# First loads reordered at the start of a two-block fp32 kernel, and the taps of the first four convolved channel pairs moved later

## What is computed

```python
def conv_ffn(hn, w_ffn_in, conv_w, conv_b, w_ffn_out, valid):
    l = hn.shape[1]
    u = jnp.where(valid[None, :, None], hn @ w_ffn_in, 0.0)
    up = jnp.pad(u, ((0, 0), (CONV_W - 1, 0), (0, 0)))
    c = conv_b + sum(conv_w[j] * up[:, j:j + l] for j in range(CONV_W))
    gate, val = jnp.split(c, 2, axis=-1)
    return (jax.nn.silu(gate) * val) @ w_ffn_out
...
    for li in range(DEPTH):
        lambda_init = 0.8 - 0.6 * math.exp(-0.3 * li)
        h = h + mixer(rms_norm(h, norm_mix_g[li]), w_in[li], w_branch[li], w_out[li], lbs[li],
                      da_lambda[li], da_subln_g[li], lambda_init, valid, pos)
        h = h + conv_ffn(rms_norm(h, norm_ffn_g[li]), w_ffn_in[li], ffn_conv_w[li], ffn_conv_b[li],
                         w_ffn_out[li], valid)
```

## Time and profile before

| | us |
|---|---|
| median of the three runs | 2747.8 |
| lowest and highest of the three | 2744.36, 2748.49 |
| the profiled execution, its own time | 2745.64 |
| its span in the trace | 2743.8 |

### The profile page before, as it was taken

The page is one execution under the profiler, slowest core; times in us unless marked ns, Lnnn a source line. Parts: engine busy times, 40 slices in busy tenths (PEclk is TensorE's granted clock), DMA queues, the critical chain, the costliest instruction groups (busy, mean ns, idle before and its releaser), DMA issues.

```text
span 2743.8 us, 49227 instructions
## 1 busy us (share of the span) xinstructions
PE 2569.7 (94%) x19196; PEld 2384.6 (87%) x19196; DVE 1468.5 (54%) x2672; ACT 1348.5 (49%) x2339; POOL 1985.1 (72%) x2181
## 2 busy tenths in 40 slices
PE   6889999998999999999998999978989998998999
PEld 6889888898999888889898998677879998778999
DVE  5876432358736874333458744645355436764540
ACT  4434444555654534445455645551255445564543
POOL 6966556797989966558798988250059999566997
PEclk8999999999999999999999999998999999999999
DMA  6433334444655433334455775120026665333665
GB/s 199 132 88 100 108 101 125 126 144 137 186 172 157 139 93 101 108 108 133 118 166 147 212 199 136 42 86 7 1 72 191 185 185 154 90 92 109 187 187 154
DMA packets 682934, 354.90 MB, mean 129 GB/s; under 512 B 11121, under 2 KB 680913, under 8 KB 682321
## 3 DMA queue, kind: packets, MB, share of 16 engines
q1 hardware_dynamic: 680464, 343.45, 43.6%
q10 hardware_dynamic: 2240, 8.31, 0.9%
HBM read 350.67 MB, written 1.05 MB: 128 GB/s over the span
## 4 chain that ended last, share of the span: by engine, by line
PE 71%; DVE 11%; POOL 8%; ACT 4%; issue 3%; DMA 2%; ACTq 0%; DVEq 0%
PE pb L276 70%; POOL wl L345 8%; ACT pool L299 1%; DVE bx L655 1%; ACT wh L334 1%; DVE xl L784 1%; DMA raw<-in_w_in 1%; DVE pool L1078 1%; PE pb L553 0%; DVE bx L790 0%; DMA raw<-in_w_ffn_in 0%; DVE bx L3265 0%; DMA raw<-in_ffn_w 0%; DVE pool L952 0%; PE pb L1309 0%
## 5 line engine op out<-in xcount | busy, mean ns | idle before, releaser
L345 POOL TENSOR_TENSOR wl<-raw,wh 128x256 fp32r<-128x256 f32 (+1 forms) x2164 | 1973.9, 948 | 748.8 <-ACT wh L334 747.5
L276 PE MATMUL pb<-xh,wh 128*128 128x272 f32 (+2 forms) x3104 | 940.9, 303 | 26.2 <-DVE pool L494 5.1
L334 ACT ACTIVATE wh<-raw 128x1024 fp32r<-128x1024 f32 (+2 forms) x669 | 689.7, 1033 | 451.6 <-PE pb L276 310.0
L276 PE MATMUL pb<-xh,wl 128*128 128x272 f32 (+2 forms) x3104 | 891.0, 287 | 0.0
L276 PE MATMUL pb<-xl,wh 128*128 128x272 f32 (+2 forms) x3104 | 891.0, 287 | 0.0
L276 PEld LDWEIGHTS pb<-xh,wh 128*128 128x128 f32 x3104 | 592.7, 191 | 52.5 <-issue 19.2
L276 PEld LDWEIGHTS pb<-xl,wh 128*128 128x128 f32 x3104 | 593.2, 191 | 3.3
L276 PEld LDWEIGHTS pb<-xh,wl 128*128 128x128 f32 x3104 | 592.2, 191 | 0.0
L276 PE MATMUL pb<-pool 128*128 128x128 f32 (+15 forms) x2064 | 325.5, 305 | 38.0 <-DVE pool L1078 14.6
L276 PEld LDWEIGHTS pb<-pool 128*128 128x128 f32 (+6 forms) x2064 | 237.6, 176 | 104.2 <-DVE pool L1078 19.8
L276 PE MATMUL pb<-u2h,wh 128*128 128x256 f32 x840 | 242.3, 288 | 5.5 <-DVE u2l L647 5.0
(11 more groups left out here) (374 smaller groups left out, 3826.7 us busy)
## 6 DMA issues: line engine op xcount, KB each, us to landing
raw<-in_w_in SPq DMA_DIRECT2D x208, 512.0 KB, 3.7
raw<-in_ffn_w SPq DMA_DIRECT2D x120, 512.0 KB, 3.8
raw<-in_w_ffn_in SPq DMA_DIRECT2D x88, 512.0 KB, 3.8
raw<-in_w_branch SPq DMA_DIRECT2D x48, 512.0 KB, 3.6
raw<-in_od_w_in SPq DMA_DIRECT2D x41, 512.0 KB, 3.8
raw<-in_w_ffn_out SPq DMA_DIRECT2D x32, 512.0 KB, 3.8
raw<-in_ev_w_in SPq DMA_DIRECT2D x20, 512.0 KB, 3.9
raw<-in_w_out SPq DMA_DIRECT2D x16, 512.0 KB, 3.6
```

What stands on the lines that cost most here:

```text
L276: return e.matmul(out, lhsT=l, rhs=r, start=a, stop=z, skip_group_check=True)
L334: E.e.activation(hi, src, ACT.Copy).then_inc(*sig("weight_hi", ("hi", g)))
L345: E.e.tensor_tensor(lo[:, s, :], src[:, s, :], hi[:, s, :].bitcast(F32), SUB).then_inc(*sig("weight_lo", *[("lo", g, i) for i in ks]))
```

## The change

At the start: the third weight piece no longer waits for `h`. Of the constants only the first three matrices (identity, ones, blocks of ones; 384 columns) are loaded at first, and the vectors right behind them; both stand ahead of the split of piece 1. The split of piece 2 moves to the middle of the squares. Lambda, the other constants (2689 columns) and the masks are requested within `a_scalars`, one at each step, and DVE turns the masks into bytes at the end of `v_scalars` instead of at its beginning, with waits `in_l` and `in2` of their own.

In each feed-forward stage of block one: for the first eight pieces there is only the scaled copy, into eight slots (`GS`, and the buffer `pbuf`); kind `cfirst`. Their taps, sigmoid, products and splits are side work `later`, in slots of their own in `rsb`, taken at rate 0.15 from the ninth piece on, four steps for each pair, sixteen in all.

```diff
@@ sp_project @@
-            if g == 2:
-                e.wait_ge(*at("in", 1))
@@ a_all_made @@
-        e.dma_start(cst[:, :], A["consts"]).then_inc(*landed("in_c", ("in_c",)))
+        c0 = cplan["p1"][0]
+        e.dma_start(cst[:, 0:c0], A["consts"][:, 0:c0]).then_inc(*landed("in_c"))
+        e.dma_start(vec[:, 8:], A["vecs"][:, 8:]).then_inc(*landed("in_c", ("in_c",)))
         a_split(E, 1)
-        e.dma_start(vec[:, 8:], A["vecs"][:, 8:]).then_inc(*landed("in2"))
-        e.dma_start(lam_in, A["lam"].broadcast_to([P, 512])).then_inc(*landed("in2"))
-        e.dma_start(POOL[:, 12288:12288 + MASKS * P], A["masks"]).then_inc(*landed("in2", ("in2",)))
-        a_split(E, 2)
         for k in range(8):
+            if k == 4:
+                a_split(E, 2)
@@ a_scalars @@
         a_logsig(E, lbt[:, 5, :], lbt[:, 0, :], "sc_a", ("sc", "l1"))
+        e.dma_start(lam_in, A["lam"].broadcast_to([P, 512])).then_inc(*landed("in_l", ("in_l",)))
         yield
         e.wait_ge(*at("sc", "m1"))
         a_logsig(E, lbt[:, 5, :], lbt[:, 4, :], "sc_a", ("sc", "l2"))
-        yield
+        c0 = cplan["p1"][0]
+        e.dma_start(cst[:, c0:], A["consts"][:, c0:]).then_inc(*landed("in2"))
+        yield
+        e.dma_start(POOL[:, 12288:12288 + MASKS * P], A["masks"]).then_inc(*landed("in2", ("in2",)))
         yield
@@ the feed-forward stage @@
+    LATER = 4
+    FIRST = [GS, PB[:, :, :].rearrange("p a b -> p (a b)").rearrange("p (a b) -> p a b", b=NT)]
+    LG, LS, LV, LP = (RSb[:, i * NT:(i + 1) * NT] for i in range(4))
+    def v_later(E, name, conv):
+        for j in range(LATER):
+            for what, dst, ch in (("g", LG, j), ("v", LV, HID // P + j)):
+                o = FIRST["gv".index(what)][:, j, :]
+                e.wait_ge(*at("tap2", name + what, j))
+                e.scalar_tensor_tensor(out=dst[:, 1:NT], in0=o[:, 0:NT - 1], ..., in1=dst[:, 1:NT], ...)
+                e.wait_ge(*last("later_v"))
+                e.scalar_tensor_tensor(out=dst[:, 2:NT], in0=o[:, 0:NT - 2], ..., in1=dst[:, 2:NT], ...)
+                yield
+            e.wait_ge(*at("gate_s", name, j))
+            e.tensor_tensor(LP, LG, LS, MLT)...
+            e.wait_ge(*last("later_v"))
+            e.tensor_tensor(LV, LV, LP, MLT)...
+            yield
+            e.wait_ge(*at("hh", name, j))
+            e.tensor_tensor(HIDL[:, j, :], LV, HIDH[:, j, :].bitcast(F32), SUB)...
+            yield
+    def v_cfirst(E, p, j, r, g):
+        v_scaled(E, p, j, r, g, FIRST["gv".index(p.name[-1])][:, j, :], ("scaled", p.name, j))
@@ glu @@
+            if conv and a == 512:
+                E.credit, later = 0.0, E.bg("later", name, conv)
+            E.run(E.part["project"](E, Proj(name + "g", ..., gate, conv=conv, **aux)), later, 0.15)
+            E.run(E.part["project"](E, Proj(name + "v", ..., val, conv=conv, **aux)), later, 0.15)
```

More of the change, by code:

```diff
@@ L1729, in program, with a_later @@
     GS = pv(20000, [4, NT])
+    LATER = 4
+    FIRST = [GS, PB[:, :, :].rearrange("p a b -> p (a b)").rearrange("p (a b) -> p a b", b=NT)]
+    LG, LS, LV, LP = (RSb[:, i * NT:(i + 1) * NT] for i in range(4))
+    def a_later(E, name, conv):
+        e, (cw, cb) = E.e, conv
+        for j in range(LATER):
+            if j:
+                e.wait_ge(*at("l_gate", name, j - 1))
+            for what, dst, ch in (("g", LG, j), ("v", LV, HID // P + j)):
+                e.wait_ge(*at("scaled", name + what, j))
+                if what == "v" and j:
+                    e.wait_ge(*at("lo_done", name, j - 1))
+                act(E, dst, FIRST["gv".index(what)][:, j, :], ACT.Identity, scale=vc(cw, 3 * ch + 2), bias=vc(cb, ch)).then_inc(
+                    *sig("later_a", ("tap2", name + what, j)))
+                yield
+            e.wait_ge(*at("taps", name + "g", j))
+            act(E, LS, LG, ACT.Sigmoid).then_inc(*sig("later_a", ("gate_s", name, j)))
+            yield
+            e.wait_ge(*at("hid", name, j))
+            e.activation(HIDH[:, j, :], LV, ACT.Copy).then_inc(*sig("later_a", ("hh", name, j)))
+            yield
@@ L1741, in v_taps @@
         e, (cw, cb) = E.e, p.aux["conv"]
-        o, freed = banks[r % 3], (("out", r),)
-        if p.aux["scaled"]:
-            v_scaled(E, p, j, r, g, GS[:, s, :], ("scaled", p.name, j))
-            e.wait_ge(*last("out_v"))
-            o, freed = GS[:, s, :], ()
+        o = banks[r % 3]
         e.wait_ge(*at("tap2", p.name, j))
@@ L1751, in v_taps @@
         e.scalar_tensor_tensor(out=dst[:, 2:NT], in0=o[:, 0:NT - 2], scalar=vc(cw, 3 * ch), in1=dst[:, 2:NT], op0=MLT,
[L1752 removed]
+                               op1=ADD).then_inc(*sig("taps", ("out", r), ("taps", p.name, j)))
     def a_cgate(E, p, j, r, g):
         name, q = p.name[:-1], j % 2
[L1756 removed]
+        if j >= LATER + 2:
             E.e.wait_ge(*at("gate", name, j - 2))
@@ L1869, in glu @@
         Wv = W.rearrange("(k p) c -> p k c", p=P)
-        E.rest, E.lo, E.conv = [], [], conv is not None
+        E.rest, E.lo, E.conv, later = [], [], conv is not None, None
         c = "c" if conv else ""
@@ L1877, in glu @@
             aux["dense"], aux["t0"] = a >= 512, t0
-            E.run(E.part["project"](E, Proj(name + "g", Wv, 8, a, 256, a // P, n, x, c + "gate", conv=conv, scaled=scaled, **aux)))
-            E.run(E.part["project"](E, Proj(name + "v", Wv, 8, HID + a, 256, a // P, n, x, c + "val", conv=conv, scaled=scaled, **aux)))
+            gate, val = ("cfirst", "cfirst") if conv and scaled else (c + "gate", c + "val")
+            if conv and a == 512:
+                E.credit, later = 0.0, E.bg("later", name, conv)
+            E.run(E.part["project"](E, Proj(name + "g", Wv, 8, a, 256, a // P, n, x, gate, conv=conv, **aux)), later, 0.15)
+            E.run(E.part["project"](E, Proj(name + "v", Wv, 8, HID + a, 256, a // P, n, x, val, conv=conv, **aux)), later, 0.15)
+        if later is not None:
+            drain(later)
         E.do("glu_end", name)
```

45 lines of the change are left out of this document (28 added, 17 removed).

## The result

The changed kernel takes **2733.96 us** (median of 15 runs, 2724.45 to 2745.71), the kernel before 2749.44 us on the same chips (15 runs, 2743.71 to 2760.21). The ratio is **0.9946, 95% interval 0.9932 to 0.9959**: 14.8 us faster, 11.3 to 18.7. The forecast was a gain of 29.3 us, to 2718.5. The profiled execution took 2729.2 us with a span of 2727.3, 16.5 us less than the earlier trace rows.

The account below looks back on a forecast made before the run. PE's matmuls were taken as the bound, gains only where PE waits or clocks lower. 10.3 + (13.2 - 2.3) + (15.3 - 7.2) = 29.3 us gained, to 2718.5 us; range 2706 to 2738.

Parts of the forecast that it names:

- Reading the kernel: Whole kernel: PE has matmuls for 2569.7 of 2743.8 us, so gains come only where it stands or clocks lower.
- The start: Program start: third weight piece requested at once, PE's sum of squares at 18.5 instead of 28.85 us, gain 10.3 us.
- The first pieces: First eight pieces of block one's feed-forward stages: only scaled copies stay, gaining 13.2 us in layer 0, 15.3 in layer 1.
- the last line of the prediction: Signs of error: moved instructions over 1.2 us, a weight piece late at 25 to 40 us, POOL pacing the first pieces.
- The later work: Dense feed-forward pieces: 28 moved DVE instructions a stage take 21.8 us, costing 2.3 us in layer 0, 7.2 in layer 1.
- were all at 1.06, 29.7: Upper bound for DVE's moved work in a dense stage: every tap and product at 1.06 us, 29.7 us in all.
- The room: DVE's idle time in dense pieces: 0.5 us a piece in layer 0, 0.33 in layer 1, plus two pieces of lateness.
- Half a POOL instruction each: Rival, dense pieces: every moved instruction waits half a POOL instruction, 1.2 us each, 33.6 a stage; 2742 us, 8%.
- Slower: Rival, dense pieces: each moved instruction waits a whole POOL instruction, 1.53 us; 2760 us, deciding from 1.30 us each; 4%.
- Long stalls move: Rival: DVE stalls like the 10.69 us one at 109.30 vanish (2711, 10%) or come among the later work (2726, 12%).
- Constants starve the weights: Rival, start: late constant and mask loads delay weight pieces by 4.3 us, or up to 12; 2723 to 2730 us, 13%.
- the start alone works: Rival: only the start gains, the taps' cost equalling their gain in the feed-forward stages; 2737 us, 3%.

Follow-up runs that it names:

- the one with PSUM: Changed kernel with the two tiles in which the moved taps are built put in free PSUM banks instead of SBUF: 2717.56 us, ratio 0.9879.
- the trace with the held tap: First trace of the changed kernel, nothing else altered, in which one moved tap of layer 1 took 7.19 us; profiled execution 2729.2 us.
- the second trace: The changed kernel run and traced once more, nothing altered: 2731.18 us, ratio 0.9934.
- the kernel with half of POOL's columns: Changed kernel with POOL forming low halves of only 64 of 128 columns per weight piece in block one's dense feed-forward pieces: 2710.99 us, ratio 0.9846.

## Why the prediction was wrong where it was

**Reading the kernel: right.** PE was the bound, and both places that the change attacks gave what stood there. The sum's matmul came at 18.65 us (18.5 forecast), no wait of ACT for a weight piece was above 1.84 us until 48 us, and PE's waits for L494 went.

**The start: right in size, and its reason narrower than told.** 10.3 us forecast, 10.0 to 11.5 in the traces at 40 us; nearly all of it is SP's wait. No trace shows a cost of the late loads. By its own runs the start alone is worth 7.1 (3.6 to 10.7) us.

**The first pieces: a little less.** 13.2 and 15.3 us forecast, 11.8 to 13.1 and 13.0 to 13.8 measured (9.5 in the trace with the held tap). In layer 0 most of the missing 1.4 us is PE at 1.2 GHz for 3.4 us from 617.1 us, after it has waited 1.1 us for the norm's sum: where the clock stays high after that wait the gain is 13.0 to 13.1. In layer 1 POOL, never idle, sets the pace, as the last line of the prediction feared: between 1418.95 and 1425.7 PE's matmuls, 0.12 us apart, come late fourteen times, by 0.07 to 0.16 us, 1.4 us together. That is inside the 0 to 1.5 us given for it (in layer 0).

**The later work: the step that failed.** "16 x 0.57 + 12 x 1.06 = 21.8 us" took the taps from the earlier trace rows and the products from the earlier trace rows. Measured were 1.15 for a tap and 1.05 for a product in layer 0, 30.9 us. The taps of the earlier trace rows were cheap because POOL had gaps where they stood, since PE waited there. The trace of before, DVE's timeline and then POOL's:

```profile
631.91 0.86 DVE L1751 SCALAR_TENSOR_TENSOR pool<-pool,vec 128x270 f32<-128x270 f32 x1
...
642.08 0.50 DVE L1751 SCALAR_TENSOR_TENSOR pool<-pool,vec 128x270 f32<-128x270 f32 x1
```

```profile
627.86 13.88 POOL L345 TENSOR_TENSOR wl<-raw,wh 128x256 fp32r<-128x256 f32 x17
642.78 3.39 POOL L345 TENSOR_TENSOR wl<-raw,wh 128x256 fp32r<-128x256 f32 x4 [1.05 <-ACT wh L334]
```

The four taps that began before 641.5, beside POOL's run without a gap, took 0.62, 0.86, 0.83 and 0.86 us, although POOL's instructions were the shorter ones there; the other twelve took 0.50 each, as POOL stood for 1.05 to 3.06 us between two pieces. The mean of 0.57 mixed the two. The moved ones stand where POOL is busy for 93 of 107 us. The products' row, beside it, had the right price for both, and the prediction's own bound "were all at 1.06, 29.7" would have been the value to take. The argument used against it, that a tap of 0.56 shows taps to be cheap, compared two conditions and not two instructions.

The room was mis-sized the other way. DVE's idle time over the whole dense part, in windows of before, of the changed kernel and of the one with PSUM:

```profile
672.00:774.00 102.00, 101.77 (x807) 101.80 (x808) 78.33 (x124) 64.18 (x105) 98.07 (x72) 1.00 0.62 180
```

```profile
650.00:757.00 107.00, 103.24 (x798) 102.09 (x797) 102.63 (x143) 67.13 (x116) 93.16 (x67) 0.98 0.56 163
```

```profile
655.00:754.00 99.00, 97.98 (x773) 97.33 (x772) 94.96 (x145) 63.74 (x111) 86.97 (x64) 1.00 0.59 169
```

The third figure is DVE's: before it was idle for 23.7 of 102 us, 0.70 a piece (807 matmuls are 33.6 pieces of 24), not 0.5; after for 4.4 of 107. Put right, the prediction's sum is 30.9 - 27 x 0.70 - 6.0 = 6.0 us lost in layer 0; measured 6.7 and 8.0. In layer 1 (19.5 us idle in 33.9 pieces, 0.575) it is 36.4 - 15.5 - 5.7 = 15.2, in the second trace, with 33.1 us of moved work, 11.9; measured 8.2 and 8.6 against the trace of before, which itself loses at least 4.7 us there, as the kernel with half of POOL's columns shows (PE waits 2.40 and 0.48 us at 1521.22 and 1529.28 and runs for 3.4 us at its lower clock): 12.9 and 13.3. The form of the sum holds within 2.3 us, its price did not.

So of the 12.8 us missing in the profiled execution (29.3 - 16.5) layer 0 has 5.8 (10.9 forecast, 5.1 measured), 4.4 of it the price of the later work and 1.4 the first pieces. Layer 1 has 6.8 (8.1 against 1.3), 5.8 in the stretch called first, of which some 3.6 is the held tap by the traces that lack it (13.0), and 1.0 in the dense one. The rest balances: the start stretch gave 1.1 more, the other stages took 1.3.

**The rivals.** *Half a POOL instruction each* had the price, 1.2 against 1.11 and 1.30, by luck in part as told above, and was given 8%; its 2742 was too slow since its room was too small. *Slower* did not come: its point was 1.30 us an instruction, and layer 1 reached just that with its held one. *Long stalls move*: both happened at once. The one of the earlier trace rows vanished (5.8 us, in the second trace too) and one came among the later work; the one near 53 us was there before, and only cost PE more. It was wrong to think that the program's order decides about these. *Constants starve the weights* and *the start alone works*: neither. (The 12.09 us of the earlier trace rows are the time of one transfer; PE's wait there was the 2.40 us just told.)

**The range** of 2706 to 2738 holds the time, near its slow end; half of the gain was missing, 29.3 - 14.8 = 14.5 us, and the forecast time was 15.5 us too low.

## What to carry to other kernels

Before a DVE instruction is moved or added, look at what POOL does where it will stand, not where its like stands now: with two SBUF inputs it costs its own 0.5 us only where POOL stands, and 1.1 to 1.6 us beside POOL's instructions of 1.45, here 1.1 us on average. Then put one input into a free PSUM bank; here that one line of tiles was worth 15 us, about as much as the whole change. Work that is put off needs a last date: find who reads its result, and when.
